# Modulation products gathered in one accumulator bank, and the inner products of the wide MLP computed with weights and activations changed over

## The reference

```python
def swiglu(x, w_in, w_out):
    gate, up = jnp.split(x @ w_in, 2, axis=-1)
    return (jax.nn.silu(gate) * up) @ w_out

# second block, for each of two layers i; s_lat and s_ctx are silu of the conditioning vectors
sh1, sc1, g1, sh2, sc2, g2 = jnp.split(s_lat @ ada_w[i] + ada_b[i], 6, axis=-1)      # 1024 -> 6144
csh1, csc1, cg1, csh2, csc2, cg2 = jnp.split(s_ctx @ ada_w[i] + ada_b[i], 6, axis=-1)
h_lat = h_lat + g2[:, None, :] * sq_relu_mlp(m_l, mlp_w1[i], mlp_w2[i])

def sq_relu_mlp(h, w1, w2):                                                     # 1024 -> 4096 -> 1024
    return jnp.square(jax.nn.relu(h @ w1)) @ w2
```

## Time and profile before

| what | before |
|---|---|
| median of 3 runs | 1997.99 us (1995.43 to 2000.47) |
| the profiled execution | 2000.63 us, span 1998.5 us |
| granted TensorE clock, mean | 0.988 |
| TensorE matmul busy | 1929.2 us, 97% |
| VectorE busy | 1144.5 us, 57% |
| ScalarE busy | 961.9 us, 48% |
| DMA | 379.68 MB, 190 GB/s |
| chain that ended last | PE 90%, DVE 5%, ACT 2% |

### The profile page before, as it was taken

The page is one execution under the profiler, slowest core; times in us unless marked ns, Lnnn a source line. Parts: engine busy times, 40 slices in busy tenths (PEclk is TensorE's granted clock), DMA queues, the critical chain, the costliest instruction groups (busy, mean ns, idle before and its releaser), DMA issues.

```text
span 1998.5 us, 23972 instructions
## 1 busy us (share of the span) xinstructions
PE 1929.2 (97%) x9559; PEld 1564.1 (78%) x9559; DVE 1144.5 (57%) x1381; ACT 961.9 (48%) x1419; POOL 111.6 (6%) x182
## 2 busy tenths in 40 slices
PE   7999999999999999999999999899999999989997
PEld 5787788778777777877877877788778877877886
DVE  5554776554475445845555646575564547655554
ACT  5445563544454444544454446453554446544442
POOL 1400001000010000000000000000100001000000
PEclk9999999999999999999999999999999999999998
DMA  9867443866657675554577664444455535234551
GB/s 297 259 219 252 157 149 118 285 232 222 222 190 255 218 243 194 187 170 160 197 251 238 204 232 158 166 171 168 130 174 189 186 128 188 85 116 155 182 190 63
DMA packets 234095, 379.68 MB, mean 190 GB/s; under 512 B 12040, under 2 KB 152720, under 8 KB 233984
## 3 DMA queue, kind: packets, MB, share of 16 engines
q1 hardware_dynamic: 231200, 369.69, 54.7%
q0 software_dynamic: 2448, 8.33, 1.6%
q10 hardware_dynamic: 336, 0.14, 0.0%
HBM read 377.06 MB, written 1.05 MB: 189 GB/s over the span
## 4 chain that ended last, share of the span: by engine, by line
PE 90%; DVE 5%; ACT 2%; issue 1%; DMA 1%; POOL 1%; SPq 0%; POOLq 0%; ACTq 0%; DVEq 0%
PE ps L450 27%; PE ps L452 26%; PE ps L451 26%; PE ps L460 5%; PE ps L576 2%; DVE w_lo L2020 1%; PE ps L627 1%; ACT w_hi L1379 1%; PE ps L609 1%; PE ps L1254 1%; PE ps L1233 1%; ACT arena L1489 1%; DVE xt_lo L2036 0%; DMA raw<-ffn_w_in_dram 0%; ACT arena L1391 0%
## 5 line engine op out<-in xcount | busy, mean ns | idle before, releaser
L2020 DVE TENSOR_TENSOR w_lo<-raw,w_hi 128x1024 fp32r<-128x1024 f32 x602 | 720.2, 1229 | 234.0 <-ACT w_hi L1379 231.4
L1379 ACT ACTIVATE w_hi<-raw 128x1024 fp32r<-128x1024 f32 x602 | 613.2, 1055 | 258.8 <-PE ps L452 231.3
L450 PE MATMUL ps<-w_hi,xt_hi 128*128 128x512 f32 x1616 | 644.1, 399 | 17.1 <-DVE xt_lo L2170 11.8
L452 PE MATMUL ps<-w_hi,xt_lo 128*128 128x512 f32 x1616 | 632.0, 391 | 0.0
L451 PE MATMUL ps<-w_lo,xt_hi 128*128 128x512 f32 x1616 | 631.1, 391 | 0.0
L450 PEld LDWEIGHTS ps<-w_hi,xt_hi 128*128 128x128 f32 x1616 | 306.6, 190 | 81.5 <-issue 20.6
L452 PEld LDWEIGHTS ps<-w_hi,xt_lo 128*128 128x128 f32 x1616 | 305.7, 189 | 64.9
L451 PEld LDWEIGHTS ps<-w_lo,xt_hi 128*128 128x128 f32 x1616 | 306.6, 190 | 61.0 <-issue 1.2
L450 PE MATMUL ps<-w_hi,ht_hi 128*128 128x512 f32 x784 | 315.8, 403 | 6.7 <-DVE ht_lo L2196 2.7
L452 PE MATMUL ps<-w_hi,ht_lo 128*128 128x512 f32 x784 | 307.9, 393 | 0.0
L451 PE MATMUL ps<-w_lo,ht_hi 128*128 128x512 f32 x784 | 307.9, 393 | 0.0
(11 more groups left out here) (265 smaller groups left out, 1094.8 us busy)
## 6 DMA issues: line engine op xcount, KB each, us to landing
raw<-mlp_w_dram SPq DMA_DIRECT2D x192, 512.0 KB, 4.3
raw<-ffn_w_in_dram SPq DMA_DIRECT2D x176, 512.0 KB, 5.8
arena<-ada_w_dram SPq DMA_DIRECT2D x96, 512.0 KB, 6.4
raw<-ffn_w_out_dram SPq DMA_DIRECT2D x88, 512.0 KB, 4.5
raw<-odd_w_in_dram SPq DMA_DIRECT2D x48, 512.0 KB, 4.8
raw<-attn_w_qkv_dram SPq DMA_DIRECT2D x24, 512.0 KB, 5.0
raw<-even_w_in_dram SPq DMA_DIRECT2D x22, 512.0 KB, 4.7
raw<-ple_w_gate_dram SPq DMA_DIRECT2D x16, 512.0 KB, 4.4
```

The lines of the kernel that those rows point to most:

```text
L450: pe.matmul(dst, a_hi, hi, start=start, stop=False)
L452: return pe.matmul(dst, a_lo, hi, start=False, stop=stop)
L1379: act.activation(w_hi[:, slot, c], raw[:, slot, c], ACT.Copy).then_inc(S(f"hi{slot}"), 1)
L2020: TT(w_lo[:, slot, c], raw[:, slot, c], w_hi[:, slot, c].bitcast(F32), ALU.subtract).then_inc(S(f"lo{slot}"), 1)
```

## The change

Four things are changed.

1. Modulation: the stationary operand is now a window into `s_pad` (54 columns wide, the two vectors in columns 22 and 23). For slab i of a run the window starts at 22 - 2i, so the two results land in rows 2i and 2i+1 of the 32, and all 12 slabs of a run add into the same 256 columns of bank 7. One ScalarE copy (`ada_row`), one `ada_turn` (two transposes) and one `ada_cols` (two sums) remain in each run. `ada_turn` stands at the run's end, now after the first six matmuls of the second row tile and not before them.
2. MLP: U(i) is `up_turned`. A 128 x 128 block of weights is the stationary operand, and 256 columns of activations (all tokens) move, so the hidden columns come out turned, four groups of 128 in banks 4 and 5: 96 matmuls of 256 columns where there were 48 of 512. `hidden` remains for step 0 only.
3. The tile of step 1 to 7 is read from h1 in SBUF, not from banks 6 and 7. `ht_hi` and `ht_lo` are made in two halves of 512 columns (ScalarE L1848, VectorE), each as soon as the slab that reads the old half is used.
4. TensorE waits for each half before the slab that needs it, and the job of a step stands ahead of that wait. VectorE's write of h1 waits until the halves before are read.

```diff
             def ada_product(g):
-                if g:
-                    pe.wait_ge(S("ada_row"), g)
+                i = g % ADA_STEPS
+                if g and i == 0:
+                    pe.wait_ge(S("ada_row"), g // ADA_STEPS)
                 pe.wait_ge(S(f"ada_in{g % 2}"), 32 * (g // 2 + 1))
                 for k in range(KT):
                     q = 32 * (k % 4)
-                    last = pe.matmul(ps[q:q + 32, 7, 0:256], s32[:, k, :], ada_raw[:, g % 2, k, :],
-                                     start=k < 4, stop=k >= 4, tile_position=(0, q))
+                    last = pe.matmul(ps[q:q + 32, 7, 0:256], s_pad[:, k, 22 - 2 * i:54 - 2 * i], ada_raw[:, g % 2, k, :],
+                                     start=i == 0 and k < 4, stop=i == ADA_STEPS - 1 and k >= 4,
+                                     tile_position=(0, q), skip_group_check=True)
                 last.then_inc(S("ada_prod"), 1)
...
                 for i in range(FFN_STEPS - 1):
                     hidden("f_", base + i, 2)
-                    ada_turn(ada + i, 256, FFN_STEPS * run + i)
                     up(4, "f_up0")
-                    pe.wait_ge(S("ada_cols"), base + i + 1)
                     ada_product(ada + i + 1)
...
                 n["epi"] += 1
-                pe.wait_ge(S("ada_row"), ada + ADA_STEPS)
-                ada_turn(ada + j, 0, FFN_STEPS * run + j)
-                ada_turn(ada + j + 1, 256, 0)
-                for k in range(2):
-                    tile_rows(1, slot, *ht(j - 1), 0, k)
+                tile_rows(1, slot, *ht(j - 1), 0, 0)
+                ada_turn(run)
+                tile_rows(1, slot, *ht(j - 1), 0, 1)
                 tile_rows(1, slot2, *ht(j), 0, 0)
                 x_fill(0)
...
+            def up_turned(j):
+                pe.wait_ge(S("m_h1"), 2 * j + 2)
+                for half in range(2):
+                    slot, uses = ring.take()
+                    for quarter in range(2):
+                        slab(slot, uses, quarter)
+                        for b in range(2):
+                            for t in (2 * quarter, 2 * quarter + 1):
+                                k = 4 * half + t
+                                for i in (2 * b, 2 * b + 1):
+                                    to = ps[:, 4 + b, i % 2 * SEQ:(i % 2 + 1) * SEQ]
+                                    c = t * 512 + i * P
+                                    hi, lo = w_hi[:, slot, c:c + P], w_lo[:, slot, c:c + P]
+                                    pe.matmul(to, hi, xt_hi[:, k, :], start=k == 0 and i % 2 == 0, stop=False,
+                                              skip_group_check=True)
+                                    pe.matmul(to, hi, xt_lo[:, k, :], start=False, stop=False, skip_group_check=True)
+                                    last = pe.matmul(to, lo, xt_hi[:, k, :], start=False, stop=k == KT - 1,
+                                                     skip_group_check=True)
+                            if k == KT - 1 and b == 0:
+                                last.then_inc(S("m_up0"), 1)
+                        last.then_inc(S(f"used{slot}"), 1)
             def mlp(job, job_read, last=False):
...
+                hidden("m_", base, 4)
                 for i in range(MLP_STEPS - 1):
-                    hidden("m_", base + i, 4)
-                    up(4, "m_up0")
-                    pe.wait_ge(S("m_ht"), base + i + 1)
+                    up_turned(base + i)
                     if i == 0:
                         acc_is_free()
+                        pe.wait_ge(S("m_ht"), 2 * base + 2)
                     job(i)
+                    pe.wait_ge(S("m_ht"), 2 * (base + i) + 1)
                     add_rows(ht_hi, ht_lo, 0, i == 0, False)
+                    pe.wait_ge(S("m_ht"), 2 * (base + i) + 2)
                     add_rows(ht_hi, ht_lo, 2, False, False)
                     job_read(i)
-                hidden("m_", base + MLP_STEPS - 1, 4)
-                pe.wait_ge(S("m_ht"), base + MLP_STEPS)
                 if last:
+                    pe.wait_ge(S("m_ht"), 2 * (base + MLP_STEPS))
                     last_rows(0, ht_hi, ht_lo, fill=False)
                     return
                 job(MLP_STEPS - 1)
+                pe.wait_ge(S("m_ht"), 2 * (base + MLP_STEPS) - 1)
                 add_rows(ht_hi, ht_lo, 0, False, False)
                 job(MLP_STEPS)
+                pe.wait_ge(S("m_ht"), 2 * (base + MLP_STEPS))
                 add_rows(ht_hi, ht_lo, 2, False, True)
...
                 def turned(j):        # ScalarE
-                    act.wait_ge(S("m_ht_ps"), 2 * j + 2)
-                    act.activation(ht_hi[:], cut(ps[:, 6:8, :].rearrange("p b n -> p (b n)"), 4, SEQ),
-                                   ACT.Copy).then_inc(S("m_ht_hi"), 1)
+                    for half in range(2):
+                        if j == base:
+                            act.wait_ge(S("m_ht_ps"), 2 * j // MLP_STEPS + half + 1)
+                        else:
+                            act.wait_ge(S("m_h1"), 2 * j + half + 1)
+                            wait_used(4 - half)
+                        act.activation(ht_hi[:, 2 * half:2 * half + 2, :],
+                                       cut(bank(6 + half) if j == base else h1[:, half, :], 2, SEQ),
+                                       ACT.Copy).then_inc(S("m_ht_hi"), 1)
...
             def ada_cols(run):        # VectorE
+                dve.wait_ge(S("ada_ps"), run + 1)
+                cols = ada_t[:, 2 * ADA_STEPS * run:2 * ADA_STEPS * (run + 1), :].rearrange("p (g t) v -> p t g v", t=2)
+                for t in range(2):
+                    src = ps[:, 7, 256 + t * P:256 + (t + 1) * P].rearrange("p (q r) -> p r q", q=4)[:, 0:2 * ADA_STEPS, :]
+                    last = dve.tensor_reduce(cols[:, t], src.rearrange("p (g v) q -> p g v q", v=2), AX_X, ALU.add)
+                last.then_inc(S("ada_cols"), 1)
```

More of the change, by code:

```diff
@@ L575, in ada_product, with ada_turn @@
                     q = 32 * (k % 4)
-                    last = pe.matmul(ps[q:q + 32, 7, 0:256], s32[:, k, :], ada_raw[:, g % 2, k, :],
-                                     start=k < 4, stop=k >= 4, tile_position=(0, q))
+                    last = pe.matmul(ps[q:q + 32, 7, 0:256], s_pad[:, k, 22 - 2 * i:54 - 2 * i], ada_raw[:, g % 2, k, :],
+                                     start=i == 0 and k < 4, stop=i == ADA_STEPS - 1 and k >= 4,
+                                     tile_position=(0, q), skip_group_check=True)
                 last.then_inc(S("ada_prod"), 1)
-            def ada_turn(g, c0, cols):
-                pe.wait_ge(S("ada_row"), g + 1)
-                if cols:
-                    pe.wait_ge(S("ada_cols"), cols)
+            def ada_turn(run):
+                pe.wait_ge(S("ada_row"), run + 1)
                 for t in range(2):
-                    last = turn(ps[:, 7, c0 + t * P:c0 + (t + 1) * P], ada_rows[:, g % 2, t * P:(t + 1) * P])
+                    last = turn(ps[:, 7, 256 + t * P:256 + (t + 1) * P], ada_rows[:, t * P:(t + 1) * P])
                 last.then_inc(S("ada_ps"), 1)
@@ L1508, in gain_of, with ada_row @@
                 return norm_t[:, c:c + KT]
-            def ada_row(g):
-                act.wait_ge(S("ada_prod"), g + 1)
-                act.activation(ada_rows[:, g % 2, :], ps[:, 7, 0:256], ACT.Copy).then_inc(S("ada_row"), 1)
+            def ada_row(run):
+                act.wait_ge(S("ada_prod"), ADA_STEPS * (run + 1))
+                act.activation(ada_rows[:], ps[:, 7, 0:256], ACT.Copy).then_inc(S("ada_row"), 1)
             def ffn(run, out0=4):
                 base = FFN_STEPS * run
-                ada = ADA_STEPS * run
                 l = run // 2
@@ L1573, in ffn @@
                     act.activation(pt_hi[:], cut(bank(5), 2, SEQ), ACT.Copy).then_inc(S("pt_hi"), 1)
-                ada_row(ada + FFN_STEPS)
+                ada_row(run)
                 if run == 3:
@@ L2170, in x2_split, with ada_cols @@
                 TT(xt_lo[:, kk, t], t_x[:, b], xt_hi[:, kk, t].bitcast(F32), ALU.subtract).then_inc(S("x2_lo"), 1)
-            def ada_cols(g, count, c0):
-                dve.wait_ge(S("ada_ps"), g + count)
-                src = ps[:, 7, c0:c0 + 256 * count].rearrange("p (t q r) -> p t r q", q=4, r=32)[:, :, 0:2, :]
-                dve.tensor_reduce(ada_t[:, 2 * g:2 * (g + count), :], src, AX_X, ALU.add).then_inc(S("ada_cols"), 1)
+            def ada_cols(run):
+                dve.wait_ge(S("ada_ps"), run + 1)
[4 more added lines that the diff above has]
+                last.then_inc(S("ada_cols"), 1)
             def ffn(run, out0=4):
                 base = FFN_STEPS * run
-                ada = ADA_STEPS * run
                 l = run // 2
@@ L2235, in ffn @@
                     xn_tile1(h_ctx, xn_c)
-                ada_cols(ada + FFN_STEPS - 1, 2, 0)
+                ada_cols(run)
                 if run % 2:
@@ L2592, in squared_relu @@
                         dve.wait_ge(S("m_relu"), 2 * j + m + 1)
```

(10 more changed lines are left out.)

13 lines of the change are left out of this document (5 added, 8 removed).

## The result

The changed kernel takes **1970.88 us** (median; 1968.70 to 1973.30) against 1996.71 us (1995.19 to 2000.47) for the one before in the same comparison: ratio 0.9868, 95% interval 0.9847 to 0.9890. That is 25.8 us, where the forecast was 20.4.

A forecast was written before the change was run, and what follows sets the result against it. TensorE, busy 97% of the span, was taken as the bound. The terms +12.8 - 15.8 - 6.8 - 1.85 - 7.9 - 0.8 + 0 = -20.4 us gave 1980.2 us, or 1978 us as a median; range 1970 to 1990.

The forecast's parts named there:

- The price of the turned product: U(i) in mlp: 96 matmuls at 0.1198 us last 11.50 us against 10.89; 21 of them add +12.8 us.
- the mixer's chunk: In the trace of before: 48 fp32r matmuls of 256 columns, each with a full load, 0.1198 us each.
- loads show through: Rival: the loads' pace sets the turned product at 0.124 to 0.129 us, 1987 to 1997 us; chance 0.07.
- loads are not hidden: Rival: loads stay unhidden in U's long run of short matmuls, slower, 2050 or 2124 us; chance 0.05.
- The steps of mlp: Six `hidden` go in each mlp's steps, 18 x 0.88 = -15.8 us, against +12.8 us for turned products.
- The ends of mlp: TensorE's waits and transposes at the mlp ends shrink: -6.8 us at the first two, -1.85 us at the third.
- So 3.41 us go twice: Ends of the first and second mlp: of 4.27 us before A(7) only 0.86 stays, -6.8 us together.
- The inner steps of ffn: In 9 of 10 steps of each run two transposes of `ada_turn` go, 36 x 0.22 = -7.9 us.
- The first steps of ffn: In each run's first step 0.2 us of TensorE's delay before `up` goes, -0.8 us for four runs.
- That wait goes, but `w_lo` takes its place: First steps of ffn: the 0.98 us wait for copy L1512 goes, but `w_lo` delays `up`; 0.2 us saved, not 1.2.
- the whole 0.98 would go in three runs, 2.9 us more: First steps of ffn, if `w_lo` came earlier: the full wait goes, 2.9 us more; kept as the low end.
- The ends of ffn: Two transposes (0.22 us) go, but `ada_turn` comes 1.36 us later: 0 for four ends, between -0.9 and +1.2 us.

The follow-up runs named there:

- e_128: The changed kernel with U's stream cut to 128 columns, 192 matmuls in place of 96, each with its load: 2222.35 us (one execution).
- e_fill: The kernel before with 18 transposes of the identity in the wait for `ht_lo` at each mlp's end: 1995.84 us, ratio 0.9990.
- e_nohalf: The changed kernel, but the first half of A's input waits for the same slab as the second: 1975.54 us, ratio 0.9891.
- e_mlp: The kernel before with the mlp part only (`up_turned`, halves of `ht_hi` and `ht_lo`, `m_h1`): 1983.63 us, ratio 0.9928.
- e_turn_first: The changed kernel with `ada_turn` ahead of the six matmuls at a run's end: 1972.77 us, ratio 0.9873.
- e_ada: The kernel before with the modulation part only: 1987.07 us, ratio 0.9943.
- e_again: The changed kernel itself, timed again beside its parts: 1969.44 us, ratio 0.9860.
- e_more: The changed kernel with the second mlp's first product turned too, so that its `hidden` goes: 1968.90 us, ratio 0.9857.
- e_both: The changed kernel with the edits of e_more and e_turn_first together: 1969.07 us, ratio 0.9857.
- e_both_fill: e_both with 22 transposes of the identity in front of the second mlp's second turned product: 1968.63 us, ratio 0.9854.
- e_row_first: The kernel before with one line moved, `ada_row` ahead of `split()` in ScalarE's order: 1991.21 us, ratio 0.9970.

## Why the forecast was right, and where it was not

*The price of the turned product* was right: 0.1198 us from the mixer's chunk and 0.120 measured, 21 x (11.52 - 10.89) = +13.2 for +12.8 us. The chunk had type, columns and load in common with U; the mixed stretch of the earlier trace rows with its 0.129, which held up the rival "loads show through", was further away. Two rivals fall with it, "loads show through" and "loads are not hidden": e_128 has pairs of load and matmul every 0.111 us. The load is recorded with 194 ns, as in the earlier trace rows, and yet one comes every 120 ns, in runs of 96. By the rule of the Trainium skill, "TensorE: Matmul & The Clock Gate", Part 3, a load overlaps matmuls in flight only if its row group differs; the trace doesn't agree, for fp32r over all row groups. The same part of that page also lets a load into the background weight buffer be pulled ahead of matmuls; that would fit the trace, but no run here shows where a load goes.

*The steps of mlp* were right: -3.6 for -3.0 us, and no wait but one of 0.3 us. The halves have the cover that the forecast gave them.

*The ends of mlp* were right as waits (-3.5 against -3.41 in the first; at the third 3.41 us down to 1.7, where 1.55 was worked out) and too small as times, by 1.7 us at the second and 1.6 behind the third. The step that failed is "So 3.41 us go twice": it prices a wait at its length. Behind that wait the clock fell in the trace of before in two cases of three, and the matmuls there ran at 0.425 us; the rows were there to be read, but I read only where A(7) starts and not what its matmuls take. These 1.6 us are in part the luck of the two executions that were profiled: 3 x 6/9 x 1.6 = 3.2 us would be the mean gain at the three ends, an estimate from the nine windows above, and e_fill's time shows 1.9. e_fill and e_nohalf bear the mechanism out, the one by a small margin.

*The inner steps of ffn* were right, -7.4 for -7.9: two transposes of 0.11 us each, with no gap near.

*The first steps of ffn* were wrong, and this is the costliest step: "That wait goes, but `w_lo` takes its place". I took the `w_lo` copy that ran at 360.72 for the one that the coming `up` needed first, because it stood next in VectorE's order. It belongs to the second of `up`'s two slabs, wanted 5.4 us after its start; the copy of the first ran from 357.12 to 359.48. I had named the other case ("the whole 0.98 would go in three runs, 2.9 us more") and turned it down; following the copies back from the first L451 of `up` to the pair that fills its slab would have shown it to be the right one. The whole wait goes in runs 1 and 2 (-1.4 each, with the two transposes), and in run 3 it was 1.51 us, not 0.98, with a clock of 0.74 over the 6 us behind it: 17.86 to 14.40 us, -3.5. Of these, 1.5 us are the clock, which stayed at 1.00 behind the same wait in e_mlp and e_fill. Without it the first steps gain 5.2 us, still 4.4 more than forecast.

*The ends of ffn* came out near the forecast, -0.4 for 0, and for the stated reason in two of four: in runs 0 and 2 TensorE waits longer for `h_lat` (0.33 us for 0.17) and gives back what it saved; runs 1 and 3 keep some 0.2 us each. With the transposes ahead of the six matmuls (e_turn_first) VectorE's sums run at 541.64 instead of 543.15, and the four ends together give 0.5 us more.

*The attention stage*, which the change doesn't touch, lasts 2.0 us longer in the profiled execution. Its wait of 2.12 us is that of the earlier trace rows, but the 32 matmuls behind it take 5.44 us instead of 3.81, at a clock of 0.72, which is 1.6 of the 2.0:

```profile
1718.87 5.44 PE L1277 MATMUL ps<-arena 128*128 128x128 f32 x32 [2.12 <-DVE arena L2732]
```

```profile
1718.00:1724.00 6.00, 5.13 (x31) 0.72 0.02 3
```

It fell in e_ada, e_again, e_more, e_turn_first, e_128, e_both and e_both_fill as well, and in e_fill, which has nothing of the change; it did not in e_mlp, e_nohalf and e_row_first. So the change isn't its cause. With it the spans differ by 27.4 us, without it they would by 29.4; the medians differ by 25.8, since the profiled execution of before lay 3.9 us above the median of its four, and that of the changed kernel 2.4 us above.

That the total fell into the range is in part luck: terms for which I had rows of the same kind came within 0.7 us each, but the two misses have one sign, 5.9 and about 3.3 us, and what works against them no term foresaw: the 2.0 us of the attention stage, and 1.6 us by which the medians differ less than the two profiled executions.

## What to carry to other kernels

When a wait goes and you name what is late next, follow that thing to the buffer and the use that it serves: a copy that runs at the right moment may serve the slab after. A wait for a small operation that stands behind larger ones in an engine's order may go by one line's move: here `ada_row` ahead of `split()` gave 6.4 us, a good half of what the whole rework of the modulation gave. And where an engine's clock depends on its being busy, price a wait with the clock behind it, read at each of its places, and compare two traces only with their mean clocks beside them.

## What the runs showed of the hardware

- TensorE's granted clock, over the 6 us behind a wait, was 0.72 behind the 2.37 us at the ends of mlp in 6 of 9 cases and behind the 2.12 us of the attention stage in 9 of 13 traces, and 1.00 in the others. Behind 1.51 us it was 0.74 in one trace of three in run 3 of ffn (before; not e_mlp, e_fill), and 1.00 at the end of the third mlp in each of eight traces. One fall costs 1.5 to 1.7 us. Executions of one kernel differ by 4.6 us (1968.70 to 1973.30) along with their mean clock (0.992 to 0.989).
- In e_128 the clock that had fallen behind the 6.0 us wait ahead of the first mlp stayed at 0.50 through the whole first U, whose matmuls of 128 columns came 0.204 us apart (49 in 10 us), and rose in the window in which matmuls of 512 columns had taken over. The same happened in the second mlp from 1540 to 1580. In the changed kernel, with 256 columns at the same place, the clock was back inside the first 10 us. The 40 us by which e_128's span grew beyond its count of matmuls stem mostly from these two stretches. Windows of 10 us in the first mlp (length, busy (count), granted clock, DMA share, GB/s), first e_128, then the changed kernel:

```profile
1275.00:1285.00 10.00, 10.00 (x49) 0.50 0.00 0
1285.00:1295.00 10.00, 10.00 (x45) 0.66 0.00 0
1295.00:1305.00 10.00, 10.00 (x60) 1.00 0.64 211
```

```profile
1245.00:1255.00 10.00, 9.76 (x68) 0.80 0.60 191
1255.00:1265.00 10.00, 10.00 (x71) 1.00 0.34 127
```

- A 128-column fp32r load with its matmul takes 0.111 us in a row of them with 128 columns moving (e_128), 0.120 with 256 (the changed kernel) and 0.227 with 512 (both kernels).
